# DVE's order in each step: the read of the step's result first, then the step's modulation products

## What is computed

```python
def _modulation(cvec, w, b):
    m = jax.nn.silu(cvec) @ w + b
    m = m[..., None, :]
    return m[..., :D_MODEL], m[..., D_MODEL:2 * D_MODEL], m[..., 2 * D_MODEL:]
```

## Time and profile before

| | us |
|---|---|
| median of 3 runs (lowest, highest) | 2297.34 (2293.23, 2301.37) |
| the profiled execution | 2291.27 |
| its span in the profile | 2289.6 |

### The profile page before, as it was taken

One profiled execution on the slowest core, in us unless ns is written; L12 is line 12 of the kernel. 1 busy time (PEld: TensorE's weight loads), 2 busy tenths in 40 slices (PEclk: granted clock), 3 DMA queues, 4 the chain that ended last, 5 costly groups with the idle time before them and its releaser, 6 DMA issues.

```text
span 2289.6 us, 43648 instructions
## 1 busy us (share of the span) xinstructions
PE 2117.3 (92%) x16374; PEld 2058.1 (90%) x16374; DVE 1555.8 (68%) x2031; ACT 883.9 (39%) x1154; POOL 169.3 (7%) x268
## 2 busy tenths in 40 slices
PE   5999987389979999999999999899999996979997
PEld 5999986368979999999999999899889996979997
DVE  4788464547879558675566758767777777667855
ACT  4333331244343333333333345315545344333442
POOL 0000000001200000000000002100000120000011
PEclk8999977569979999999999999999999998989998
DMA  4568521005748568785587756446435882536752
GB/s 172 183 234 278 185 83 46 0 1 178 263 151 272 195 223 274 240 274 194 201 271 261 274 193 213 169 163 212 143 134 200 270 272 95 183 115 226 264 183 93
DMA packets 119549, 434.04 MB, mean 190 GB/s; under 512 B 13216, under 2 KB 13600, under 8 KB 119216
## 3 DMA queue, kind: packets, MB, share of 16 engines
q1 hardware_dynamic: 90672, 328.11, 42.0%
q0 software_dynamic: 28800, 104.87, 13.1%
HBM read 430.83 MB, written 2.10 MB: 189 GB/s over the span
## 4 chain that ended last, share of the span: by engine, by line
PE 83%; DVE 12%; issue 2%; ACT 2%; DMA 1%; POOL 0%; DVEq 0%; SPq 0%; POOLq 0%; ACTq 0%
PE ps L474 24%; PE ps L475 24%; PE ps L476 24%; DVE w_lo L1186 2%; PE ps L534 2%; PE ps L529 1%; DVE mod_sum L1202 1%; PE ps L820 1%; PE ps L830 1%; PE ps L571 1%; DVE sq L1255 1%; PE ps L540 1%; PE ps L702 1%; DVE rstd L1247 0%; DVE a_lo L1263 0%
## 5 line engine op out<-in xcount | busy, mean ns | idle before, releaser
L908 ACT ACTIVATE w_hi<-raw 128x1024 fp32r<-128x1024 f32 x610 | 635.0, 1057 | 715.0 <-PE ps L476 704.5
L474 PE MATMUL ps<-a_hi,w_hi 128*128 128x256 f32 x3024 | 864.2, 286 | 46.6 <-DVE w_lo L1186 22.8
L475 PE MATMUL ps<-a_lo,w_hi 128*128 128x256 f32 x3024 | 861.1, 285 | 0.0
L476 PE MATMUL ps<-a_hi,w_lo 128*128 128x256 f32 x3024 | 860.8, 285 | 0.0
L1186 DVE TENSOR_TENSOR w_lo<-raw,w_hi 128x1024 fp32r<-128x1024 f32 x610 | 740.5, 1256 | 130.3 <-ACT w_hi L908 127.7
L474 PEld LDWEIGHTS ps<-a_hi,w_hi 128*128 128x128 f32 x3024 | 583.7, 193 | 50.5 <-issue 24.6
L475 PEld LDWEIGHTS ps<-a_lo,w_hi 128*128 128x128 f32 x3024 | 583.8, 193 | 0.0
L476 PEld LDWEIGHTS ps<-a_hi,w_lo 128*128 128x128 f32 x3024 | 583.6, 193 | 0.0
L474 PE MATMUL ps<-b_hi,w_hi 128*128 128x256 f32 x1920 | 554.2, 289 | 18.9 <-DVE w_lo L1186 7.6
L475 PE MATMUL ps<-b_lo,w_hi 128*128 128x256 f32 x1920 | 547.3, 285 | 0.0
L476 PE MATMUL ps<-b_hi,w_lo 128*128 128x256 f32 x1920 | 547.2, 285 | 0.0
(11 more groups left out here) (269 smaller groups left out, 1336.7 us busy)
## 6 DMA issues: line engine op xcount, KB each, us to landing
raw<-w_main SPq DMA_DIRECT2D x610, 512.0 KB, 4.3
side<-w_side POOLq DMA_DIRECT2D x200, 512.0 KB, 4.5
x_tok<-x_in SPq DMA_DIRECT2D x4, 512.0 KB, 6.1
ctx_tok<-ctx_tok SPq DMA_DIRECT2D x1, 2048.0 KB, 10.2
y_out<-o_tok SPq DMA_DIRECT2D x4, 512.0 KB, 2.7
cons<-cons_in SPq DMA_DIRECT2D x1, 542.0 KB, 8.1
table<-counts_tab SPq DMA_DIRECT2D x1, 512.0 KB, 11.0
table<-masks_in SPq DMA_DIRECT2D x1, 448.0 KB, 12.3
```

Source lines behind the costliest of these rows:

```text
L474: pe.matmul(out_ap, wh, act_hi[:, kt, :], start=first and n == 0, stop=False)
L475: pe.matmul(out_ap, wh, act_lo[:, kt, :], start=False, stop=False)
L476: mm = pe.matmul(out_ap, wl, act_hi[:, kt, :], start=False, stop=last and n == len(blocks) - 1)
L908: act.activation(w_hi[:, slot, :], raw[:, slot, :], ACT.Copy).then_inc(hi_ready, 1)
```

## The change

In `reading`'s `body` the loop of `add_mod` moves behind the wait and the read. Everything else stays: the same instructions, the same semaphores, the same program of the other engines. It takes effect in the first 16 steps (8 in `ev_kv`) of the 12 stages with products; in the others the loop is empty.

```diff
                     if chain is not None:
                         next(chain)
+                    dve.wait_ge(halves_used, i * 4 + (2 * s + 2))
+                    read(i, k, s % 2)
                     for e in range(each if k < DT else 0):
                         add_mod(stage, i, each * k + e)
-                    dve.wait_ge(halves_used, i * 4 + (2 * s + 2))
-                    read(i, k, s % 2)
```

## The result

The changed kernel takes 2334.68 us (median of 4, 2329.43 to 2336.75); the kernel before, on the same chip, 2298.78 (median of 4, 2293.23 to 2301.37). The ratio is 1.0154, with a 95% interval of 1.0134 to 1.0174: 35.9 us slower. The forecast was 2336 with a range of 2314 to 2346, so both hold.

The account below looks back on a forecast made before the run. PE was taken as the bound, busy inside the stages and not waiting for the reads. Terms 16.0 + 15.6 + 5.8 + 1.8 = 39.2 us on profiled 2291.27 gave 2330.5, plus 6 to the median: 2336, range 2314 to 2346.

Parts of the forecast that it names:

- L529 later at five ends: Ends of down0, down1, ev_kv, ev_z, od_z: L529 waits for read and products, 2.1 to 3.7 us each, sum 16.0.
- clock at these ends: After the idle at the five ends, low clock in L529 and next first steps: 15.6 us, bounds 0 and 15.6.
- Pool's queue: In out and ev_out side load 15 precedes the last square's add, so L508 is late: 2.9 and 1.8; sum 5.8.
- attention in `ev_z`: Products enter the DVE/ACT ring for three slots, silu to silu 11.2 instead of 9.96; PE sees 1.8 us, bounds 0, 3.8.
- inside the stages: Steps inside the stages: products move behind the read and w_lo comes later, within slack; cost 0, bounds 0 to 13 us.
- the doubtful one: End of down1: the clock loss of 3.4 us was least certain there, its idle being the shortest at 2.1 us.
- Rival (a): At the new ends the granted clock holds, so 15.6 + 1.1 us go: 2319; chance 0.2, in full or for most ends.
- The covers: Slack before PE wants the first w_lo: 1.3 us in down0, 0.8 to 1.0 in out, 0.35 in up0 behind a gate.
- Rival (b): DVE becomes the bound in two-vector stages, 0.2 us over in all 64 steps: +13, 2349; chance 0.1.
- Rival (c): Late reads, in the attention, cost now: gain 0.5 us, 2297 if ends cost nothing; chance 0.06, of it 0.01 faster.
- Adding 6 us for the profiled execution: Whole kernel: profiled 2291.27 becomes 2330.5; the runs' median, 2297.34, lies 6 above the profiled one, so 2336 was predicted.

Follow-up runs that it names:

- second profile: The kernel before, no edit, profiled once more: 2301.86 us, span 2300.1.
- the reversed last step alone: The kernel before, but in the last step of every stage the read goes first, then the products: 2331.56 us, ratio 1.0139.
- the waits filled: The changed kernel with added fp32 matmuls, results unused, on PE ahead of L529 at the five ends where it waits: 2321.85 us, ratio 1.0104.
- two kernels with freed ends: Against the kernel before: norm ahead of sums, seven other sums inside next first steps; old order 2286.91 us; new order, Pool's squares first, 2288.93.

## Why the prediction was right, point by point

The account is made from the starts of the steps in the changed kernel against those of the kernel before in its second profile: 34.9 us between the spans.

| | forecast | measured |
|---|---|---|
| L529 later at five ends | 16.0 | 15.4 |
| clock at these ends: L529 and the step behind | 15.6 | 13.9 |
| Pool's queue (`out`, `ev_out`) | 5.8 | 6.1 |
| attention in `ev_z` | 1.8 | 1.7 |
| inside the stages | 0 | 0 |
| a low stretch of the clock in `od_u` that the kernel after lacks | - | -1.5 |
| smaller pieces, in `down2`, `od_u` and ahead of `out` | - | -0.7 |
| sum | 39.2 | 34.9 |

**Idle at the ends.** One by one PE is idle for 3.03, 1.83, 3.50, 2.98 and 3.29 us, 14.6 in all, where 3.3, 2.1, 3.7, 3.3 and 3.6 were forecast. But the forecast counted from L529's former start, which lies 0.16 before the end that the profile gives the last matmul, while the idle time counts from that end. Counted as in the forecast, from the start of the last step on, L529 comes 3.2, 2.0, 3.65, 3.1 and 3.45 later, 15.4 in all. What is left of the excess, 0.1 at each end, is the issue that I put between operations. The rows of DVE above show none: a read of 0.42 starts at 946.87, and the product starts 0.34 later, before the read's end as the profile gives it. In `ev_q` there was no wait, as said. That this is the cause is shown twice: the reversed last step alone brings the loss (2331.56), and moving only the sums takes the five waits away (2306.23).

**The clock.** For L529 and the first step together, against the second profile of before: `down0` 2.96 - 1.19 = 1.8 (forecast 2.0), `down1` 0.46 + 2.67 = 3.1, `ev_kv` 1.74 + 1.45 = 3.2, `ev_z` 0.11 + 1.49 = 1.6, `od_z` 1.65 + 2.58 = 4.2 (forecast 3.4 each). The sum, 13.9, is near the upper bound that I took, but the single terms are not what I said, and that they come out so near is partly luck: `ev_z` lost half of its 3.4 and `od_z` 0.8 more, and the first step of `up1`, costed at nothing, was 1.2 faster than before. I put 1.6 on L529 and 1.8 on the step each time. The forecast set out from the first step of `down1`, 5.84 us at a granted clock of 1.00 behind 16 L529 without idle time. In fact L529 after a wait of 2.98 us was still fast (1.95 us, clock 1.00) and after 1.83 us partly slow (2.30, 0.81), and the step behind it took 7.4 to 8.6 (0.78 to 0.65). `down1`, called the doubtful one for its short idle, lost as much as `ev_kv` with the longest. What sets the moment of a fall the traces don't show: the same idle of 2.98 and 2.99 us at the same place led to L529 of 1.95 and 3.15 in two kernels. Rival (a) would have needed first steps at 5.95 and a clock of 1.00, as at four of these ends in the second profile of before, and there was none. That idle is the cause of most of it and not the changed order as such: with the waits filled 11.5 us came back.

**Pool's queue.** In `out` L508 started after 4.66 us idle instead of 1.98: 2.7 later (forecast 2.9), 3.3 with slower matmuls in front of the norm (L508 1.22 instead of 0.70, L529 6.83 instead of 6.64). In `ev_out` 3.45 instead of 1.88: 1.6 (forecast 1.8); with a slower L508 (1.22 instead of 0.70) and L529 (3.41 instead of 1.84), and less time in the norm's sums, 2.8 (forecast 2.9, of it 1.1 for L529 at 3.4 instead of the 2.32 of the earlier trace rows). The exchange of Pool's two calls takes both back to 2.4 us idle. It doesn't reach 1.98, because the last add, 0.71 long before, lies beside DVE's products there (632.94 to 635.88) and takes longer, 1.23 (Pool, squares first):

```profile
633.56 1.23 POOL L441 TENSOR_TENSOR sq_sum<-sq_sum,sq_tile 128x256 f32<-128x256 f32 x1 [2.56 <-ACT sq_tile L919]
```

**Attention.** From silu to silu in `ev_z` the profile after has 11.07 us, where 11.2 was forecast and 9.96 stood before:

```profile
1744.96 0.38 ACT L895 ACTIVATE sg<-ps 128x256 f32<-128x256 f32 x1
...
1756.03 0.38 ACT L895 ACTIVATE sg<-ps 128x256 f32<-128x256 f32 x1
```

What PE sees of it, 1.8 between bounds of 0 and 3.8, was a choice for which the forecast shows no working; that 1.7 was measured is partly luck.

**Inside the stages.** The covers held, and were a little thicker than forecast. In `down0` and `rest` the first `w_lo` is ready 1.47 us before PE wants it (forecast 1.3), in `out` 1.48 (0.8 to 1.0), in `up0` behind a gate 0.52 (0.35). DVE in `up0`, where the step ends at 709.55 and 715.31:

```profile
709.84 0.42 DVE L1572 TENSOR_TENSOR gated<-ps,sg 128x256 f32<-128x256 f32 x1 [0.76 <-PE ps L476]
...
711.17 2.47 DVE L1202 SCALAR_TENSOR_TENSOR mod_sum<-side,csil,mod_sum 128x1024 f32<-128x1024 f32 x2
713.57 2.35 DVE L1186 TENSOR_TENSOR w_lo<-raw,w_hi 128x1024 fp32r<-128x1024 f32 x2
```

The first `w_lo` is done at 714.79. Rival (b) named `out` as the place that would break first, and it is the narrowest:

```profile
587.02 0.42 DVE L1559 TENSOR_TENSOR res<-ps,res 128x256 f32 x1
...
589.75 2.90 DVE L1186 TENSOR_TENSOR w_lo<-raw,w_hi 128x1024 fp32r<-128x1024 f32 x2
592.78 0.42 DVE L1559 TENSOR_TENSOR res<-ps,res 128x256 f32 x1
```

From read to read 5.76 us, PE's own step, and no idle time between the operations: DVE has less than 0.15 us to spare in a step. The extra time of `w_lo` beside Pool's add (590.72 to 591.56) falls on the second half (1.76 us, the first 1.22), which PE wants 2.9 us later, so it doesn't thin the first half's 1.48. No wait of registers showed between read and product.

**Rival (c)** said that the late reads are what costs now. The two kernels with freed ends refute it: 2286.91 with the old order and 2288.93 with the new, so the early read gains nothing even where the ends cost nothing.

**From the sum to the median.** Adding 6 us for the profiled execution was in the right direction, though too little: the profile of before was some 10 us quicker than a typical one. The forecast is 1.3 above the measured median for two reasons that partly cancel: 39.2 against the 35.9 between the medians is 3.3 too much, and the median of before that I added it to (2297.34) is 1.4 below the one in the comparison (2298.78); the rest is rounding.

## What to carry to other kernels

Reordering work on an engine that isn't the bound was free here in the middle of the loop (0 us inside the stages), where its slack covered the move (0.5 us was left at the narrowest), and was paid in its last turn (15.4 us), where the bound engine runs straight into a consumer of what was moved back: look there first, and count the clock that falls with the idle time as a second cost, here of about the same size (13.9 beside 15.4). The cure here was to give the bound engine other dense work between the loop's end and that consumer (2306.23 instead of 2334.68), and to keep long rows of light matmuls short (behind two of 16 the clock was 1.00, behind one of 32 it was 0.77). The largest gain here was found by asking what else stands behind the late sums: a read of them ahead of a norm, which cost the kernel before 9.1 us by the trace and 11.7 by the medians.

## What was not expected of the hardware

- Single executions of the same kernel were 10 to 15 us quicker than the others (before: 2284.82 among 13 of some 2300; profiled spans of 2289.6 and 2300.1). Of the 10.5 us between the two profiles 7.9 lie in the first layer's attention, some 230 us long, at a clock of 0.65 instead of 0.63. A gain or loss under 10 us should not be read from one pair of profiles without looking at that stretch.
- PE's first step behind the ends took 7.40 to 8.62 us, while the earlier trace rows had made me think of 7.6 as the worst. An idle time of only 0.78 us with 16 sums behind it stood ahead of a slow step at one end (7.10 us at 0.80), where 0.70 us at another did not (5.83 at 1.00).
- Thirty-two matmuls of one column, 3.6 us in a row, were followed by a lower clock with PE never idle (0.77 in the step behind); the same 32 in two rows of 16, with 24 dense matmuls between, were not (1.00).
- A gain ahead of a wait was lost in it: 1.7 us earlier into the end of `ev_z` gave 1.6 back through the clock.
